# First mixture of experts: experts taken in order of their row counts, the last four in two packs of 64 slots

## The reference, cut to what matters

```python
D_FF_EXPERT = 1408; N_EXPERTS = 8; TOP_K = 2
logits = (xt @ w_router) + b_router            # 256 x 8
top_v, top_i = lax.top_k(logits, 2)
gates = softmax(top_v)
for e in range(8):
    y = y + dense_gate[:, e:e+1] * ((silu(xt @ w1[e]) * (xt @ w3[e])) @ w2[e])
```

## Time and profile before

| | us |
|---|---|
| median of 3 runs | 1565.21 |
| their range | 1563.22 to 1569.49 |
| span of the profiled execution (first to last instruction) | 1561.5 |
| S5 mixer and router until the first expert matmul | to 558.9 |
| first MoE, first expert matmul to last combining matmul | 558.9 to 963.0 |
| next mixer and its routing | 963.0 to 1083.3 |
| second MoE | 1083.3 to about 1520 |
| last gate and store | to 1561.5 |

### The profile page before, as it was taken

One profiled execution on the slowest core, in us unless ns is written; L12 is line 12 of the kernel. 1 busy time (PEld: TensorE's weight loads), 2 busy tenths in 40 slices (PEclk: granted clock), 3 DMA queues, 4 the chain that ended last, 5 costly groups with the idle time before them and its releaser, 6 DMA issues.

```text
span 1561.5 us, 24697 instructions
## 1 busy us (share of the span) xinstructions
PE 1494.5 (96%) x10596; PEld 1127.9 (72%) x10596; DVE 1005.6 (64%) x1441; ACT 697.2 (45%) x915; POOL 36.5 (2%) x34
## 2 busy tenths in 40 slices
PE   7999999999999999999999998999999999999897
PEld 7988879989898888888888887986434443443335
DVE  5777787999968698888988888775121221212127
ACT  5673346554443576767777674453101111110114
POOL 0000110000020000000000001000000000000001
PEclk9999999999999999999999999999999999999999
DMA  9441045454631569989899897389999999999991
GB/s 343 161 159 57 2 155 205 159 188 180 230 109 37 209 222 361 351 321 358 326 349 346 322 344 281 129 351 378 428 427 428 427 427 427 428 427 427 426 412 43
DMA packets 37841, 443.45 MB, mean 284 GB/s; under 512 B 5600, under 2 KB 6112, under 8 KB 10464
## 3 DMA queue, kind: packets, MB, share of 16 engines
q1 hardware_dynamic: 36576, 438.35, 70.8%
q10 hardware_dynamic: 1152, 3.46, 0.6%
HBM read 440.75 MB, written 1.05 MB: 283 GB/s over the span
## 4 chain that ended last, share of the span: by engine, by line
PE 79%; DVE 11%; DMA 6%; ACT 2%; issue 2%; PEldq 0%; ACTq 0%; DVEq 0%; PEld 0%
PE psum L237 77%; DMA sb_spare<-moe_up 3%; DMA sb_work<-moe_up 2%; DVE sb_ring_r L1276 2%; DVE sb_work L2786 1%; PE psum L2119 1%; PE psum L2571 1%; DVE sb_work L1370 0%; DVE sb_ring_r L520 0%; DVE sb_work L1368 0%; DVE sb_split L2064 0%; DVE sb_work L1369 0%; DMA sb_front<-conv_w 0%; DVE sb_work L2784 0%; PE psum L404 0%
## 5 line engine op out<-in xcount | busy, mean ns | idle before, releaser
L2064 DVE TENSOR_TENSOR sb_split<-sb_ring,sb_split 128x2048 fp32r<-128x2048 f32 (+1 forms) x144 | 301.2, 2110 | 46.1 <-ACT sb_split L2058 45.2
L237 PE MATMUL psum<-sb_work 64*64 64x64 f32 (+11 forms) x3392 | 281.4, 331 | 19.2 <-DVE sb_work L2786 7.8
L2058 ACT ACTIVATE sb_split<-sb_ring 128x2048 fp32r<-128x2048 f32 (+1 forms) x144 | 253.0, 1773 | 90.8 <-PE psum L237 52.9
L237 PE MATMUL psum<-sb_split 128*128 128x512 f32 (+1 forms) x912 | 268.8, 384 | 0.4 <-DVE sb_split L2378 0.4
L237 PEld LDWEIGHTS psum<-sb_work 128*64 128x64 f32 (+4 forms) x3392 | 147.7, 142 | 136.5 <-issue 117.1
L237 PE MATMUL psum<-sb_split,sb_lnp_r 128*128 128x512 f32 (+1 forms) x768 | 230.5, 374 | 1.5 <-DVE sb_split L2347 1.5
L237 PEld LDWEIGHTS psum<-sb_split 128*128 128x128 f32 x912 | 169.8, 188 | 30.9 <-DVE sb_split L2378 0.9
L237 PEld LDWEIGHTS psum<-sb_split,sb_lnp_r 128*128 128x128 f32 x768 | 142.7, 188 | 21.8 <-DVE sb_split L2347 1.7
L237 PE MATMUL psum<-sb_xT_r,sb_ring_r 128*128 128x256 f32 x512 | 143.9, 283 | 0.0
L2784 DVE TENSOR_TENSOR sb_work<-sb_work,psum 128x512 f32<-128x512 f32 x16 | 11.0, 689 | 166.9 <-ACT sb_work L2696 166.9
L2696 ACT ACTIVATE sb_work<-psum 128x512 f32<-128x512 f32 x16 | 9.6, 598 | 239.7 <-PE psum L237 239.7
(11 more groups left out here) (475 smaller groups left out, 2660.4 us busy)
## 6 DMA issues: line engine op xcount, KB each, us to landing
sb_ring<-moe_wide SPq DMA_DIRECT2D x48, 2048.0 KB, 8.8
sb_work<-moe_up SPq DMA_DIRECT2D x33, 2048.0 KB, 25.6
sb_ring<-w_dense SPq DMA_DIRECT2D x23, 2048.0 KB, 8.5
sb_ring<-moe_last SPq DMA_DIRECT2D x24, 1536.0 KB, 8.4
sb_ring<-moe_up SPq DMA_DIRECT2D x18, 2048.0 KB, 25.3
sb_work<-moe_down SPq DMA_DIRECT2D x17, 2048.0 KB, 23.9
sb_ring<-ffn_wide SPq DMA_DIRECT2D x14, 2048.0 KB, 7.7
sb_ring<-moe_down SPq DMA_DIRECT2D x9, 2048.0 KB, 25.0
```

What stands on the lines that cost most here:

```text
L237: return nc.tensor.matmul(o, lhsT, rhs, start=start, stop=stop, **kw)
L2058: act.activation(wh[half_home(e, i)][:, 0:half_size(i)], half_raw(e, i), ACT.Copy).then_inc(sem("m1_high"), 1)
L2064: v.tensor_tensor(wl[home][:, 0:half_size(i)], half_raw(e, i), wh[home][:, 0:half_size(i)].bitcast(F32), ALU.subtract).then_inc(sem("m1_sp ...
```

## The change

Eight things are changed, all for the first MoE.

1. The experts are ranked by their number of rows (`ordered`, seven small VectorE instructions after the ranks' matmul), and everything that had an expert's number now has a position in this order: ranks and gates are permuted by a 0/1 matrix (`by_position`).
2. SyncE reads the expert at a position from SBUF into a register and uses it in the address of the loads.
3. Positions 0 to 3 stay as before: 128 slots, split products. Positions 4 to 7 are two packs of two experts with 64 slots each, in plain float32, the two experts' matmuls in the two halves of the array's columns. The six members run in the order 0, 1, (4, 5), 2, 3, (6, 7).
4. There are three gathers instead of four (both packs share one) and four combines, two of which have half the matmuls.
5. Weights of packs aren't split, nor their activations.
6. Loads are of half units (1 MiB, 0.75 or 0.5 MiB) to ten half homes: six in `ring` and four where `wl` was. The low part is written over the raw half. A home is released when PE has used it.
7. `low_rows(0)` goes from VectorE to GpSimd. The splits of the first expert's weights that stood in the S5 mixer are gone; the first gather comes before them.
8. A pack expert overflows over 64 rows instead of 128.

```diff
+        MEMBERS = ((0,), (1,), (4, 5), (2,), (3,), (6, 7))
+        FIRST_PACKED = 4
+        PAIR_BEGINS, GATHERS, COMBINES = (0, 2, 3), (1, 2), (2, 3, 5)
+        M1_HOMES = (2, 3, 4, 5, 0, 1, 6, 7, 8, 9)
+        M1_LOADS = [(m, i, j) for m in range(len(MEMBERS)) for i in range(NH) for j in range(len(MEMBERS[m]))]
...
+        def split_high(act, m, i):
+            half_loaded(act, m, i)
...
+            act.activation(half_high(m, i), half_raw(m, i), ACT.Copy).then_inc(sem("m1_high"), 1)
+        def split_low(v, m, i):
+            v.wait_ge(sem("m1_high"), half_number(m, i) + 1)
+            v.tensor_tensor(half_low(m, i), half_raw(m, i), half_high(m, i).bitcast(F32), ALU.subtract)\
+             .then_inc(sem("m1_split"), 1)
...
             def up(m, name, o):
...
+                    if packed(m):
+                        for j in range(PACK):
+                            half_loaded(pe, m, i, j)
+                        for k in range(DC // 2):
+                            kk = DC // 2 * ab + k
+                            for j in range(PACK):
+                                r, s0 = slice(SLOTS2 * j, SLOTS2 * (j + 1)), P * (m // 3) + SLOTS2 * j
+                                ins = mm(o[r, 0:n], x_packs[:, kk, s0:s0 + SLOTS2], half_raw(m, i, j)[:, n * k:n * k + n],
+                                         kk == 0, kk == DC - 1)
...
+            def ordered():
+                v.wait_ge(sem("rank_ps"), 1)
+                dve_link(v, v.scalar_tensor_tensor(order_key, bank[1][:, 0:EXPERTS], float(EXPERTS), iota8, ALU.mult, ALU.subtract))
+                dve_link(v, v.tensor_tensor(order_gt, bc(order_key, 1, EXPERTS), bc(order_key, 2, EXPERTS), ALU.is_gt))
+                dve_link(v, v.tensor_reduce(order_at, order_gt, AX.X, ALU.add))
...
+                v.tensor_copy(order_i[:, :], order_ids).then_inc(sem("order_ready"), 1)
...
+            def packed_member(m):
+                outputs(m)
+                combined(m, 0, 1, 2, 3)
+                hidden(m, 0)
+                hidden(m, 1)
...
+                sp.wait_ge(sem("order_ready"), 1)
+                expert_at = {}
+                for n, (m, i, j) in enumerate(M1_LOADS):
+                    position = MEMBERS[m][j]
+                    if position not in expert_at:
+                        expert_at[position] = sp.value_load(order_i[0:1, position:position + 1], min_val=0, max_val=EXPERTS - 1)
+                    if n >= len(M1_HOMES):
+                        m1_load_used(sp, n - len(M1_HOMES))
...
+                    sp.dma_start(half_raw(m, i, j), src[:, words]).then_inc(sem(f"home_loaded{n % len(M1_HOMES)}"), 16)
```

More of the change, by code:

```diff
@@ new lines, in split_member @@
+            def split_member(m):
+                if m > 0:
+                    outputs(m)
+                high(m, 3, 4, 5)
+                silu(m, 0)
+                high(m, 6, 7, 8)
+                turned(m, 0)
+                high(m, 9)
+                silu(m, 1)
+                high(m, 10, 11, 12, 13, 14)
+                turned(m, 1)
+                high(m, 15)
+                silu(m, 2)
+                if m in PAIR_BEGINS:
+                    slots_turned(m)
+                    gates(m)
+                high(m, 16, 17)
+                if m in GATHERS:
+                    for i in range(3):
+                        gathered(m, i)
+                turned(m, 2)
+                if m in GATHERS:
+                    gathered(m, 3)
+                if not packed(m + 1):
+                    high(m + 1, 0, 1, 2)
@@ new lines, in packed_member @@
+            def packed_member(m):
+                outputs(m)
+                silu(m, 0)
+                turned(m, 0)
+                silu(m, 1)
+                turned(m, 1)
+                silu(m, 2)
+                if m in PAIR_BEGINS:
+                    slots_turned(m)
+                    gates(m)
+                if m in GATHERS:
+                    for i in range(3):
+                        gathered(m, i)
+                turned(m, 2)
+                if m in GATHERS:
+                    gathered(m, 3)
+                if m < LAST_MEMBER:
+                    high(m + 1, 0, 1, 2)
@@ new lines, in packed_member @@
+            def packed_member(m):
+                outputs(m)
+                combined(m, 0, 1, 2, 3)
+                hidden(m, 0)
+                hidden(m, 1)
+                if m in GATHERS:
+                    v.wait_ge(ped, M1_PE[m, "gs"])
+                    selected(1)
+                hidden(m, 2)
+                if m in GATHERS:
+                    for i in range(4):
+                        gathered(m, i)
+                if m < LAST_MEMBER:
+                    low(m + 1, 0, 1, 2)
@@ L2388, in moe1_vector @@
-            selected(0)
-            low_rows(1)
+            dve_link(v, by_position(rank1, mask1))
+            dve_link(v, v.tensor_scalar(rank1[:, 0:EXPERTS, :], rank1[:, 0:EXPERTS, :], 1.0, None, ALU.subtract))
+            selected(0)
+            low_rows(v, 1)
+            for i in range(2):
+                gathered(-1, i)
+            low(0, 0)
+            for i in range(2, 4):
+                gathered(-1, i)
             low(0, 1)
-            for i in range(4):
-                gathered(-1, i)
+            weighted()
```

640 lines of the change are left out of this document (357 added, 283 removed).

## The result

The changed kernel takes 1517.61 us (median of 4 runs, 1516.38 to 1519.3), the kernel before 1565.25 (4 runs, 1563.22 to 1569.49): a ratio of 0.970, 95% interval 0.968 to 0.971, so 47.6 us faster. The forecast was 1498, a gain of 67.4: the direction is right, the gain is 20 us too large. The time lies inside the stated range (1486 to 1528), but outside the forecast's own bounds (1486 to 1510), in the part that was kept for rival A. The profiled execution has a span of 1514.8 us (1561.5 before), which is 46.7 less.

A forecast was written before the change was run, and what follows sets the result against it. The prediction took PE's work in the first MoE as the bound: 324.7 us of it, plus 6 for starting and 6 for steady loads, less 404.1 gives -67.4, so 1498 us. Range 1486 to 1528.

The forecast's parts named there:

- rival A: First MoE: loads become the bound, still faster than before; 1523 us at 380 GB/s; chance 0.17.
- PE's work, before and after: First MoE: PE's matmuls, transposes, gathers and combines fall from 404.1 us to 324.7, so 79.4 us go.
- my terms: First MoE: PE's work summed from split members, packs, gathers, combines and turning: 324.7 us.
- Rival C: Packs: the array's halves don't work side by side with weights from different homes; 1607 us; chance 0.04.
- B: First MoE: loads so slow, from 342 GB/s down, that the kernel is slower; 1578 us at 330; chance 0.05.
- Loads, start: First MoE's start: loads wait for the order, PE starts 2.7 late, fourth half later; +6 us (0 to +12).
- Loads, steady: First MoE's packs: homes full, PE stays the limit, waits only where homes are nearly empty; +6 us (0 to +12).
- The rate, weighed: First MoE's loads: 427 GB/s taken for the packs, 380 kept as the other end.
- My own sign between the two: Packs: PE waiting for `home_loaded` over 12 us in all would show the loads as bound, the forecast wrong.
- After the stage: Behind the first MoE: next mixer's loads land around PE's end and are wanted some 16 us later.
- Rival D: First MoE: the change does less because a pack's expert overflows; emptiest have 62, 54, 54, 53 rows; no chance.

The follow-up runs named there:

- e4: Changed kernel with the expert order written in as numbers, so six half units load before routing ends, ring homes first in turn: 1526.05 us.
- e3: Changed kernel with only a quarter of each packed half unit loaded (short last ones a half), same matmuls, result not the reference's: 1496.94 us.
- e2: Changed kernel with the second MoE's 2 MB units loaded as two 1 MB loads, 8 KB rows instead of 16: 1525.87 us.
- e5: Changed kernel with the last pack's last down projection taking its first half once that half's loads are there: 1517.91 us.
- e1: Changed kernel with GpSimd's subtraction for the first rows' low parts waiting until the expert list is in integers: 1518.59 us.

## Why the prediction was right, and where it failed

- *PE's work, before and after: right.* A pair of a pack's matmuls takes what the earlier trace rows promised: 32 records, which are 8 pairs, take 7.04 us in the first pack, 0.87 us a pair and the tail of the last. With small loads the stage takes 331.3 us from the first expert's matmul, against 328.0 from my terms (324.7, and the 3.3 of the start that lie behind that matmul); the 3 us over are mostly the last pack, 65.7 where I had 62. (The prediction's "24 k-steps of gate and up with 512 columns twice over" should read 16, twice over; the sum has the right 32.) Rival C (1607 us) has fallen. So has B: no stretch that held PE up was below 400 GB/s.

```profile
694.37 7.04 PE L238 MATMUL psum<-sb_work 128*64 128x512 f32 x32
```

- *Loads, start (+6): too small by 2 to 3 us, and for a reason that I had ruled out.* The first expert began 5.6 us late instead of 2.7. The selection was ready at 556.3 instead of 554.1, and 1.8 us of that is the conversion that GpSimd holds up; I took it at 0.2 us, and called `low_rows` on GpSimd free, since it was "done before it is needed". The rest came behind it, where the granted clock fell to 0.79 from 560 to 570. I had also asked when the first load lands; e4 shows that loads already in SBUF start nothing earlier, since the selection and the place of the splits in ScalarE's order decide.

- *Loads, steady (+6): the step that failed, and it is mis-sized by 13 us.* "More than the homes hold, so they are full. The pack needs 34.6 MB, 24.1 of them during its 67 us of PE: 56.4 us. Not bound." e3 prices the loads of both packs at 19 us in the stage. Two numbers in the step are wrong. First, full homes are not ten loads landed. At the first pack's first matmul nine of its loads had been issued and seven had landed, 8.5 MB in all with what was on its way (43.1 moved, 34.6 used), not 10.5; at the second pack's 8.0 MB (111.8 less 103.8). Second, the rate with full queues was 418 to 420, not 427.

- *What this means for each pack.* The second needed 34.6 - 8.0 = 26.6 MB, 63.3 us at 420. Beside its last loads 1.2 MB of the mixer's weights moved too, so the last one landed 66.2 us after the pack's start, where PE has work for 57.6 (e3): 7.8 us of waits and the clock behind them. The first needed 26.1 MB, 62.4 us at 418, which is still less than its 67 us of PE. There PE waited only 1.7 us for the pack's own loads. But when the next expert's first half had landed, at 736.25 and 70.8 us after the pack's start, 28.6 MB had moved: the pack's 26.1, that half's 1.05 and 1.4 of the loads behind it; and from the pack's start to 700 the rate was 389, not 418, which costs 2.4 us. The homes were then nearly empty, as I had said for this point: ScalarE and VectorE needed 4.3 us to split that half, and PE stood for 3.9. The split was in my +6, the waits of the second pack and the clock were not.

```profile
665.50:700.00 34.50, 34.50 (x161) 13.18 (x162) 5.54 (x8) 2.95 (x5) 0.00 (x0) 1.00 0.97 389
690.00:736.30 46.30, 44.38 (x249) 19.74 (x247) 4.88 (x10) 5.53 (x12) 0.00 (x0) 1.00 1.01 418
```

- *The 20.7 us by which the gain was missed, in all:* 12.8 for the packs' loads (18.8 us instead of 6), 2.9 before the first expert's matmul, 3.3 in the stage without them (e3 against my terms), 1.7 behind the stage.

- *The rate, weighed: near.* 427 was taken, 380 kept as the other end, and it was 418 with full queues. I named "halves of 8 KB per partition instead of 16" for rival A, and e2 shows that it counts, though only for 2%. A's own arithmetic at 418 gives 551 + 331 + 6 = 888, 26 us before the true end at 914.6: the loads do not bound the stage as a whole. In the split experts they stand still with full homes, 327 to 405 GB/s between 610 and 690, and what they miss there is what the packs lack. The stage is bound by PE in one half and by loads in the other, which is neither the forecast nor A. My own sign between the two, over 12 us of waits for `home_loaded` in the packs, did not decide either: 9.5 us by PE's direct waits, 13.4 with the split behind the first pack. That the time fell inside the range is owed to the width that A had added to it.

- *After the stage: nearly right.* "They are wanted some 16 us later" left out the norm's rows behind them, 1.1 us. The same wait, grown to 6.5 us, ate e5's whole gain.

- *Rival D* had no chance and none was seen.

## What to carry to other kernels

Where a stage alternates between stretches with more work than loads and stretches with more loads than work, add up each stretch by itself: its bytes, less what has *landed* (not what has been issued) when it begins, by the rate of loads of that form, and look at what the next stretch needs first. Price a wait of PE with the clock that follows it, not by its length alone. A buffer more is then worth about its size by the rate in every such stretch (here 2 to 3 us for 2.5), unless it is taken from a buffer that the other stretches need. And before an instruction is called hidden on GpSimd, look at which of VectorE's operations stand beside it.

## What the runs showed of the hardware

A GpSimd subtraction holds some operations of VectorE and not others. Beside it a conversion of 8 elements took 1.97 us instead of 0.17 and a pair of 128 x 512 operations with two tensors from SBUF 3.50 instead of 1.41, while a reduction of one tensor took its usual 0.22 and norm statistics 1.27 for two. The operation held ends just behind GpSimd's end, 0.03 us in the conversion and 0.55 us in the pairs. Where a pair had begun just before GpSimd (e1), its first operation took the usual 0.74 us, its second 2.84, and GpSimd's subtraction 2.78 instead of 2.35, so GpSimd seems to be held as well. The Trainium skill, "SBUF — State Buffer", Who interferes with whom, says that the two engines share a pair of ports, that whoever comes first has it for a whole instruction while the other is blocked, and that VectorE's casts (in a mode with two ports) and its instructions with two SBUF inputs can meet GpSimd there, its reductions never. The trace agrees: 1.97 and 2.84 us for what was held, 0.22 for the reduction. This rule, which I did not weigh in the prediction, would have pointed at the 1.8 us.

One core's loads move 418 GB/s in loads of 1 MB with 8 KB in a row and 425 in loads of 2 MB with 16 KB, with full queues in both.
